# Prompt attention of a hybrid decoder: two heads in row halves of TensorE, probabilities weighted before their transposes, outputs summed in one PSUM bank

## The chip, the cores and the metric

The kernel runs as one program on one core of a Trainium2 chip. The metric is the device time in microseconds (us), the median of several runs. A profile of one execution goes with it; TensorE's granted clock is given there as a share of 2.4 GHz (0.50 is 1.2 GHz). All data is f32.

## The reference

One step through two trunk layers. Every layer runs two token mixers, on a prompt of 512 tokens and on a sample part of 8 sequences of 8 new tokens, then an MLP. What matters here is the prompt's attention:

```python
q_a, kv_c, kv_s, kv_w, gate, q_b, kv_b = _project(h, w_in)
kvc = _compress(kv_c, pe, w1, w2)                       # 31 compressed keys and values
o_cmp, o_sel = lax.map(lambda qp: _nsa_global(qp[0], qp[1], kvc, blocks, slopes_a), (qb, posb))
o_win, _ = _local_attn(q_a, kv_w[:, :, 0], kv_w[:, :, 1], slopes_a, WIN_A - 1, 1.0)
o_dil = _dilated_prompt(q_b, kv_b, slopes_b)
...
o_a = jnp.einsum('bthdc,bthc->bthd', o_a, gate)         # three branches, a gate for each
return jnp.concatenate([o_a.reshape(B, T, -1), o_dil.reshape(B, T, -1)], axis=-1) @ w_out
```

Eight sparse heads (two KV groups of four) attend to three sets of keys: compressed, selected and window. Each branch has its own softmax, and the three outputs are added with sigmoid gates. Eight dilated heads have one softmax each, whose bias holds the counts of the three dilations. Every score has an ALiBi bias. With 512 tokens every causal block is among the selected, so the selected branch is plain causal attention too.

## The kernel before

The order of work is written out by hand for each engine; engines meet at semaphores. A layer has the input projection, the prompt's attention, the sample part (8 batches), and the output projection with the MLP. The change lies in the prompt's attention.

It runs in four rounds (`g`). A round takes a pair of sparse heads (one of each KV group, 64 channels each, lying in the two halves of the 128 partitions) and a pair of dilated heads. Its 32 steps (`m`) are one head, one branch, one tile of 128 queries: 24 sparse (head 0 and head 1, each compressed, selected, window, four tiles each) and 8 dilated. Tile `t` sees 128 (t+1) keys; a compressed step has 32. GpSimd makes a copy of the pair's queries for each head, in which the other head's half is zero (`queries`), so that a score product over all 128 partitions gives one head.

A step goes through the engines thus. TensorE, `step_scores` (L1132): scores of up to 512 keys into bank `m % 2`. VectorE, `step_bias` (L1662): one pass adds the bias, stores the negated result to `p_sb` (four slots) and leaves the row minimum in `stat`. ScalarE (L673): exponential, with the row sum. TensorE, `step_transposes` (L1142, L1145): 128-column transposes into bank `2 + m % 2`. ScalarE (L683): copy to `p_pt`. TensorE, `step_outputs` (L1155, L1160): the transposed probabilities are stationary, and the values of both heads (128 columns) stream. VectorE, `step_add` (L1670 to L1686): reciprocal of the row sum, times the gate, and the head's 64 columns are added to `og` (or stored to `ogd`). TensorE's queue has scores(m), transposes(m-2), outputs(m-4). At a round's end eight transposes (`pair_transposes`, L1165) turn `og` and `ogd`, and VectorE copies them to `hT`.

VectorE makes the bias tables of the next part meanwhile (`sparse_bias` L1635, L1636; `dilated_bias` L1641). The sync queue loads the first window tiles (L502) once the projection is stored, and the dilated keys and values (L505 to L509) once `og_k` says that all pairs are kept. Then the sample part starts: L1229 compresses its pages, L1248 are the dilated scores.

## Time and profile before

| | us |
|---|---|
| median of 3 runs | 2600.89 (2598.64 to 2602.43) |
| profiled execution | 2606.01 |
| its span, first to last instruction | 2604.2 |
| TensorE busy in the span | 2444.6 |
| VectorE, ScalarE, GpSimd busy | 1007.6, 617.1, 504.0 |
| mean granted clock | 0.966 |

The span is what the trace covers; the execution's own time has some 2 us around it. A busy TensorE is an array with some matmul in it, not one at its peak: a matmul's record lasts from its start until its last column has left the array, so the starts of two neighbours show what it costs.

### The profile page before, as it was taken

What the parts mean: (1) busy time and instruction counts of PE and PEld (TensorE: products, weight loads), DVE (VectorE), ACT (ScalarE), POOL (GpSimd) and SP (SyncE); (2) the same over time, 40 slices, a digit from 0 to 9 for tenths busy, and PEclk for the clock granted to TensorE, in tenths of its full rate; (3) what the DMA queues carried; (4) which work ended last, traced back from release to release, by engine and by line L of the source; (5) the groups of instructions that cost most, each with busy time, mean ns of one, the idle gap of its engine ahead of it and who ended that gap; (6) DMA issues with size and microseconds to landing.
All of it is one profiled execution on the core that took longest, in us unless ns stands there. A gap on an engine that the chain in (4) does not pass through costs nothing.

```text
span 2604.2 us, 44706 instructions
## 1 busy us (share of the span) xinstructions
PE 2444.6 (94%) x13806; PEld 1755.5 (67%) x13806; DVE 1007.6 (39%) x3023; ACT 617.1 (24%) x1562; POOL 504.0 (19%) x511
## 2 busy tenths in 40 slices
PE   7998999898979999999999989999898789999998
PEld 4545777676756777777745466676676667777776
DVE  2002776434335332335500137753434352323374
ACT  2101555111112331221101026531111123232202
POOL 0001010000004343444200011100000233433340
PEclk8997999999989999999999979999999899999999
DMA  8633001787774344544365310037777553544541
GB/s 326 214 124 93 1 0 43 280 299 263 270 269 188 152 182 157 210 167 178 126 241 177 134 51 1 0 142 287 251 290 267 223 188 151 197 180 158 202 167 37
DMA packets 126229, 448.23 MB, mean 172 GB/s; under 512 B 17665, under 2 KB 89218, under 8 KB 104962
## 3 DMA queue, kind: packets, MB, share of 16 engines
q1 hardware_dynamic: 116464, 416.45, 43.3%
q10 hardware_dynamic: 9618, 29.98, 3.3%
q8 instruction: 72, 1.18, 0.2%
q14 instruction: 75, 0.61, 0.1%
HBM read 435.76 MB, written 152.57 MB: 226 GB/s over the span
## 4 chain that ended last, share of the span: by engine, by line
PE 84%; DVE 5%; issue 4%; DMA 4%; ACT 1%; SPq 1%; DVEq 0%; ACTq 0%; POOLq 0%
PE bank L969 35%; PE bank L1052 15%; PE bank L1229 8%; PE bank L1132 4%; DMA zone<-in_dilated_k 3%; PE bank L1160 3%; PE bank L1340 3%; PE bank L1248 2%; PE bank L1145 2%; PE bank L1373 1%; PE bank L1155 1%; PE bank L950 1%; DVE zone L1662 1%; PE bank L1068 1%; PE bank L1342 1%
## 5 line engine op out<-in xcount | busy, mean ns | idle before, releaser
L969 PE MATMUL bank<-zone,ring 128*128 128x288 f32 x1664 | 424.8, 407 | 8.0 <-DVE zone L1516 5.4
L1052 PE MATMUL bank<-ring,hT 128*128 128x512 f32 (+3 forms) x960 | 399.5, 571 | 7.9 <-ACTq L694 5.1
L969 PEld LDWEIGHTS bank<-zone,ring 128*128 128x128 f32 x1664 | 314.8, 190 | 101.0 <-DVE zone L1516 10.8
L969 PE MATMUL bank<-zone,w 128*128 128x288 f32 x1408 | 353.5, 406 | 0.0
L969 PEld LDWEIGHTS bank<-zone,w 128*128 128x128 f32 x1408 | 267.5, 190 | 73.9
L1052 PEld LDWEIGHTS bank<-ring,hT 128*128 128x128 f32 (+1 forms) x960 | 170.9, 183 | 204.2 <-issue 190.0
L1229 PE MATMUL bank<-ring,w 128*128 128x128 f32 x2048 | 239.6, 277 | 0.6 <-DMA ring<-in_cache_kv_cmp 0.6
L1229 PEld LDWEIGHTS bank<-ring,w 128*128 128x128 f32 x2048 | 232.1, 192 | 3.1 <-issue 2.4
L818 POOL TENSOR_TENSOR w<-ring 128x512 f32<-128x512 f32 x72 | 97.4, 1352 | 544.7 <-PE bank L969 310.9
L673 ACT ACTIVATE zone<-zone,stat 128x32 f32<-128x32 f32 (+4 forms) x256 | 128.4, 502 | 164.2 <-DVE stat L1662 162.2
L610 ACT COPY zone<-bank 128x288 f32<-128x288 f32 x72 | 28.7, 398 | 562.0 <-PE bank L969 562.0
L1132 PE MATMUL bank<-zone 128*128 128x512 f32 (+3 forms) x384 | 149.3, 472 | 0.2
L1160 PE MATMUL bank<-zone 128*128 128x128 f32 (+1 forms) x960 | 141.4, 279 | 0.3
L889 POOL TENSOR_TENSOR zone<-constants,stat 128x1024 f32<-128x1024 f32 x16 | 30.3, 1895 | 565.0 <-DVE stat L1860 565.0
L969 PE MATMUL bank<-xT,ring 128*128 128x288 f32 x512 | 135.2, 407 | 2.0 <-ACT zone L610 2.0
L1160 PEld LDWEIGHTS bank<-zone 128*128 128x128 f32 x960 | 123.0, 193 | 8.0 <-issue 6.8
L1662 DVE CUSTOM_DVE_ANT_0 zone<-bank,zone 128x32 f32<-128x32 f32 (+4 forms) x256 | 106.5, 416 | 35.9 <-PE bank L1132 22.2
L969 PEld LDWEIGHTS bank<-xT,ring 128*128 128x128 f32 x512 | 96.8, 190 | 29.3 <-ACT zone L610 2.9
L821 POOL TENSOR_TENSOR w<-w,ring 128x512 f32<-128x512 f32 x72 | 109.7, 1523 | 13.5 <-POOL w L818 13.5
L1248 PE MATMUL bank<-zone 128*32 128x128 f32 (+1 forms) x1664 | 67.8, 286 | 45.3 <-DMA zone<-in_dilated_k 45.3
L602 ACT ACTIVATE ring<-ring,gains 128x256 f32<-128x256 f32 x256 | 105.3, 495 | 0.0
L825 POOL TENSOR_TENSOR w<-ring,w 128x512 f32<-128x512 f32 x72 | 99.9, 1388 | 12.8 <-POOL ring L822 11.6
(240 smaller groups left out, 2890.9 us busy)
## 6 DMA issues: line engine op xcount, KB each, us to landing
out_dil_s<-in_state_kv_dil SPq DMA_DIRECT2D x48, 2720.0 KB, 12.0
ring<-in_w_units SPq DMA_DIRECT2D x72, 1024.0 KB, 4.8
zone<-in_dilated_v SPq DMA_DIRECT2D x16, 3328.0 KB, 11.2
ring<-in_cache_kv_cmp SPq DMA_DIRECT2D x256, 128.0 KB, 2.7
ring<-in_cache_kv_sel SPq DMA_DIRECT2D x256, 128.0 KB, 5.7
ring<-in_w_in SPq DMA_DIRECT2D x10, 2048.0 KB, 8.0
zone<-in_dilated_k SPq DMA_DIRECT2D x16, 1280.0 KB, 5.9
zone<-in_dilated_k SPq DMA_DIRECT2D x16, 1024.0 KB, 8.0
```

Of the source, the lines that this page charges most:

```text
L602: last = nc.scalar.activation(w_[:, h, k], w_[:, h, k], ACT.Copy, scale=gain_of(l * 2 + 1, 4 * h + k))
L673: nc.scalar.activation(p_sb[:, m % 4, 0:w], p_sb[:, m % 4, 0:w], ACT.Exp, scale=-1.0, bias=stat[:, 16 + m % 4:17 + m % 4], accum_out=stat[ ...
L818: nc.gpsimd.tensor_tensor(c_[:, 0], w_[:, 2], w_[:, 3], ALU.add).then_inc(s_comb.sem, 1)
L821: nc.gpsimd.tensor_tensor(c_[:, 1], c_[:, 0], w_[:, 0], ALU.subtract).then_inc(s_comb.sem, 1)
L825: nc.gpsimd.tensor_tensor(c_[:, 2], w_[:, 1], c_[:, 1], ALU.subtract).then_inc(s_comb.sem, 1)
L969: last = mm(dst[:, 0:HALF], lhs[:, k, :], rhs(k), start=first and k == 0, stop=(k == 3), skip_group_check=True)
L1052: last = mm(dst, hT[:, k, t * P:t * P + ROWS[t]], ring[:, n % 2, k * CH:k * CH + width], start=start and k == 0, stop=stop and k == KT - 1)
L1132: mm(bank[m % 2][:, 0:w], q[:, m % 4 * P:(m % 4 + 1) * P], kT[:, 0:w], start=True, stop=True).then_inc(a_s.sem, 1)
L1160: last = mm(dst, p_pt[:, m % 2, c * P:(c + 1) * P], v, start=(c == 0), stop=(c == w // P - 1))
L1229: last = mm(out[:, k, first:first + P], w1[:, s, j, :], rawt[:, :, s, k, j % 8, :], start=(j == 0 and k == 0), stop=(j == 15 and k == 1), ...
L1248: return mm(S[32 * g:32 * g + M, e * P:(e + 1) * P], strips[:, a, at:at + M], tile[:, p * P:(p + 1) * P], start=(j == 0 and p == 0), stop= ...
L1662: V.tensor_tensor_reduce(p_sb[:, m % 4, 0:w], bank[m % 2][:, 0:w], bias, -1.0, BIG, ALU.add, ALU.min, stat[:, 16 + m % 4:17 + m % 4]).then ...
```

## The change

A slot now has both heads of a pair, so a round has 12: selected, window and dilated, four tiles each. The two score products use 64 partitions each, at their own halves of the array's rows, and write to two banks; zeroed copies of the queries are gone. After the exponential VectorE takes the reciprocals of both row sums, and GpSimd multiplies the probabilities with reciprocal and gate (`weigh`) before they are transposed. ScalarE copies the first head's transposed probabilities, VectorE the second's; each head has one bank for them. For the outputs the values are stationary (128 rows, 64 columns) and the probabilities stream, the two heads at the two column halves; selected, window and compressed branch add up in bank 6, the dilated one is in bank 7, and ScalarE copies both to `hT` already turned. So `step_add` and `pair_transposes` go. The compressed branch of a pair is one block: four score products, softmax on 256 columns, four transposes, one output product of 512 columns. Its buffers lie where the projection was staged, so TensorE first waits for those stores, and the first window load waits for the end of the last round. 

```diff
-STEPS_A, STEPS_D = 24, 8
+STEPS_A, STEPS_D = 8, 4
 STEPS, ROUNDS = STEPS_A + STEPS_D, 4
-AHEAD = 4
+AHEAD, TO_T, TO_PV = 4, 3, 4
...
+        p_q, p_qd = part(10240, SEQ), part(10752, SEQ)
...
+        p_sb = part(W + 2048, 4, 2, SEQ)
+        p_kd = part(W + 7168, SEQ)
...
+        p_c, p_ptc, p_vd = part(stg_at, 4, 2, 32), part(stg_at + 256, SEQ, rows=slice(0, 64)), part(stg_at + 768, 4, P)
+        p_pt = [part(W + 6144, 2, SEQ), part(stg_at + 1280, 2, SEQ)]
...
+                sp.wait_ge(og_d.sem, og_d.at(l, ROUNDS))
                 load_window(0)
-                sp.wait_ge(og_k.sem, og_k.at(l, 8))
...
+            def step_probs(l, g, m):
+
+                n, w, slot = g * STEPS + m, step_keys(m), m % 4
+                for k in range(2):
+                    act.wait_ge(a_sb.sem, a_sb.at(l, 2 * n + k + 1))
+                    at = 2 * slot + k
+                    nc.scalar.activation(
+                        p_sb[:, slot, k, 0:w], p_sb[:, slot, k, 0:w], ACT.Exp, scale=-1.0,
+                        bias=stat[:, 16 + at:17 + at], accum_out=stat[:, 32 + at:33 + at]).then_inc(a_e.sem, 1)
+
+            def keep_first_head(l, g, m):
+
+                n, w = g * STEPS + m, step_keys(m)
+                act.wait_ge(a_t.sem, a_t.at(l, 2 * n + 1))
+                if not isinstance(n, int) or n >= 2:
+                    act.wait_ge(a_o.sem, a_o.at(l, n - 1))
+                copy(p_pt[m % 2][:, 0, 0:w], bank[4][:, 0:w]).then_inc(a_pt[0].sem, 1)
...
+                        step_probs(l, *in_round(g, m))
+                    if m == 6:
+                        act.wait_ge(c_b.sem, c_b.at(l, g + 1))
+                        nc.scalar.activation(p_c, p_c, ACT.Exp).then_inc(c_e.sem, 1)
+                    if m >= TO_T and (m - TO_T < STEPS or not ends):
+                        keep_first_head(l, *in_round(g, m - TO_T))
+                    if m == 9:
+                        act.wait_ge(c_t.sem, c_t.at(l, g + 1))
+                        copy(p_ptc, bank[7][low, :]).then_inc(c_k.sem, 1)
+                    if m == 11:
+                        keep_pair(l, g, g, bank[6], STEPS_A).then_inc(og_a.sem, 1)
+                    if m == STEPS + TO_PV - 1:
+                        keep_pair(l, g, g + 4, bank[7], STEPS).then_inc(og_d.sem, 1)
...
+                def weigh(g, m):
+
+                    n, w, slot = g * STEPS + m, step_keys(m), m % 4
+                    pool.wait_ge(a_w.sem, a_w.at(l, n + 1))
+                    pool.sem_inc(waits_taken_pool, 1)
...
+                        p = p_sb[:, slot, k, 0:w]
+                        inverse = sm[:, 2 * slot + k:2 * slot + k + 1]
+                        if m < STEPS_A:
+                            last = nc.gpsimd.tensor_scalar(p, p, inverse, p_gate[:, m % 4, k, 1 + m // 4:2 + m // 4],
+                                                           ALU.mult, ALU.mult)
+                        else:
+                            last = nc.gpsimd.tensor_scalar(p, p, inverse, None, ALU.mult)
+                        last.then_inc(a_n.sem, 1)
...
+                    for m in range(STEPS):
+                        weigh(g, m)
+                        if m == 1:
+                            pool.wait_ge(a_s.sem, a_s.at(l, g * STEPS))
+                            pool.sem_inc(waits_taken_pool, 1)
+                            pair_copy(p_kd, kbT[:, ds(g, 1), :])
+                            pair_copy(p_qd, qbT[:, ds(g, 1), :]).then_inc(a_q.sem, 1)
+                        if m == 3:
+                            pool.wait_ge(a_o.sem, a_o.at(l, g * STEPS))
+                            pool.sem_inc(waits_taken_pool, 1)
+                            nc.gpsimd.tensor_copy(p_vd, vst[:, :, ds(256 + g * P, P)]).then_inc(a_q.sem, 1)
+                        if m == 6:
+                            pool.wait_ge(c_w.sem, c_w.at(l, g + 1))
+                            pool.sem_inc(waits_taken_pool, 1)
+                            nc.gpsimd.tensor_tensor(
+                                p_c.rearrange("p t k n -> p (t k) n"), p_c.rearrange("p t k n -> p (t k) n"),
+                                sm[:, 56:64].unsqueeze(2).to_broadcast([P, 8, NCK_P]), ALU.mult).then_inc(c_n.sem, 1)
+                        if m == 9 and more:
+                            pool.wait_ge(a_s.sem, a_s.at(l, g * STEPS + STEPS_A))
+                            pool.sem_inc(waits_taken_pool, 1)
+                            pair_copy(p_q, qaT[:, ds(g + 1, 1), :]).then_inc(a_q.sem, 1)
+
...
+                n, w, t = g * STEPS + m, step_keys(m), m % 4
+                q, kT = (p_q, (ksT, kwT)[m // 4]) if m < STEPS_A else (p_qd, p_kd)
...
+                for k, rows in enumerate((low, high)):
+                    last = mm(bank[2 * (m % 2) + k][:, 0:w], q[rows, t * P:(t + 1) * P], kT[rows, 0:w], start=True, stop=True)
+                last.then_inc(a_s.sem, 1)
+
+            def step_transposes(l, g, m):
+
+                n, w, slot = g * STEPS + m, step_keys(m), m % 4
+                for k in range(2):
+                    pe.wait_ge(a_n.sem, a_n.at(l, 2 * n + k + 1))
+                    if not isinstance(n, int) or n >= 1:
+                        pe.wait_ge(a_pt[k].sem, a_pt[k].at(l, n))
                     pe.sem_inc(waits_taken_pe, 1)
+                    for c in range(w // P):
+                        last = tr(bank[4 + k][:, c * P:(c + 1) * P], p_sb[:, slot, k, c * P:(c + 1) * P], ident[:])
+                    last.then_inc(a_t.sem, 1)
...
+                for c in range(w // P):
+                    for k, rows in enumerate((low, high)):
+                        if m < STEPS_A:
+                            at = m // 4 * P + k * HD
+                            v, B, first = vst[:, c, at:at + HD], bank[6], m == 0
+                        else:
+                            v, B, first = p_vd[:, c, k * HD:(k + 1) * HD], bank[7], m == STEPS_A
+                        last = mm(B[rows, t * P:(t + 1) * P], v, p_pt[m % 2][:, k, c * P:(c + 1) * P], start=first and c == 0,
+                                  stop=(c == w // P - 1), skip_group_check=True)
                 last.then_inc(a_o.sem, 1)
...
+                    last = mm(bank[7][:, t * 64:(t + 1) * 64], p_q[:, t * P:(t + 1) * P], ktcp[:].rearrange("p k n -> p (k n)"),
+                              start=(t == 0), stop=(t == 3), skip_group_check=True)
...
+                    last = tr(bank[7][low, t * P:(t + 1) * P], p_c[:, t].rearrange("p k n -> p (k n)"), ident[:])
...
+                mm(bank[6][:], vcp[:], p_ptc, start=False, stop=True, skip_group_check=True)
...
+                    if m == 5:
+                        chunk_scores(l, g)
+                    if m >= TO_T and (m - TO_T < STEPS or not ends):
+                        step_transposes(l, *in_round(g, m - TO_T))
+                    if m == 9:
+                        chunk_probs_transposes(l, g)
+                    if m >= TO_PV:
+                        step_outputs(l, g, m - TO_PV)
+                    if m == 10:
+                        chunk_outputs(l, g)
...
+                for k in range(2):
+                    at = 16 + 2 * slot + k
+                    V.tensor_tensor_reduce(
+                        p_sb[:, slot, k, 0:w], bank[2 * (m % 2) + k][:, 0:w],
+                        (p_bias if m < STEPS_A else p_biasd)[:, k, SEQ - w:SEQ], -1.0, BIG,
+                        ALU.add, ALU.min, stat[:, at:at + 1]).then_inc(a_sb.sem, 1)
...
+                out, sums = sm[:, 2 * slot:2 * slot + 2], stat[:, 32 + 2 * slot:34 + 2 * slot]
+                V.reciprocal(out, sums).then_inc(a_w.sem, 1)
...
+                V.tensor_copy(p_pt[m % 2][:, 1, 0:w], bank[5][:, 0:w]).then_inc(a_pt[1].sem, 1)
...
+                V.tensor_tensor(v, bank[7][:, 0:256].rearrange("p (a n) -> p a n", a=8),
+                                p_biasc.rearrange("p t k n -> p (t k) n"), ALU.add).then_inc(order.sem, 1)
...
+                V.tensor_reduce(sm[:, 40:48], v, X, ALU.max).then_inc(order.sem, 1)
...
+                V.tensor_tensor(v, v, sm[:, 40:48].unsqueeze(2).to_broadcast([P, 8, NCK_P]), ALU.subtract).then_inc(c_b.sem, 1)
...
+                V.tensor_reduce(sm[:, 48:56], p_c.rearrange("p t k n -> p (t k) n"), X, ALU.add).then_inc(order.sem, 1)
...
+                V.reciprocal(sm[:, 48:56], sm[:, 48:56]).then_inc(order.sem, 1)
...
+                V.tensor_tensor(sm[:, 56:64], stat[:, 40:64].rearrange("p (a e) -> p a e", e=3)[:, :, 0], sm[:, 48:56], ALU.mult).then_inc(c_w.sem, 1)
...
+                    if m >= 1 and (m - 1 < STEPS or not ends):
+                        step_weights(l, *in_round(g, m - 1))
...
+                    if m == 5:
+                        chunk_bias(l, g, order)
+                    if m == 7:
+                        chunk_weights(l, g, order)
...
+                    if m >= TO_T and (m - TO_T < STEPS or not ends):
+                        keep_second_head(l, *in_round(g, m - TO_T))
```

**The order on TensorE.** A sparse step whose scores have 512 keys, before (names: `bank` is PSUM, `zone` the work buffer in SBUF; a row of a matmul against f32 data is two records in the trace):

```order
L1132 MATMUL bank<-zone 128x512 [waits scores_biased]
L1145 MATMUL bank<-c_ident,zone 128x128 [waits probsT_kept,probs]
L1145 MATMUL bank<-c_ident,zone 128x128
L1160 MATMUL bank<-zone 128x128 [waits outputs_added,probsT_kept]
L1160 MATMUL bank<-zone 128x128 x3
```

And now the slot of such scores, with the end of the slot before it ahead:

```order
L1212 MATMUL bank<-zone 64x128 x5
L1177 ISA
L1180 MATMUL bank<-zone 128x512 [waits scores_biased]
L1180 MATMUL bank<-zone 128x512
L1187 ISA
L1189 REGISTER_ALU [waits probs_weighted]
L1192 MATMUL bank<-c_ident,zone 128x128 [waits first_head_kept]
L1187 ISA
L1192 MATMUL bank<-c_ident,zone 128x128 [waits probs_weighted,second_head_kept]
L1212 MATMUL bank<-zone 64x128 [waits first_head_kept,second_head_kept]
L1212 MATMUL bank<-zone 64x128 x7
```

The next score product stands behind outputs that wait for both copies; the transposes are now those of m-3, and wait for GpSimd's `probs_weighted` and for the copy of the step before.

**The order on VectorE.** The step with 384 keys, before, in a sparse branch:

```order
L1660 ISA [waits probs_transposed]
L1662 ISA zone,stat<-bank,zone 128x384 [waits scores]
L1662 ISA stat 128x1
L1670 RECIPROCAL sm<-stat 128x1 [waits outputs]
L1671 ISA
L1681 ISA [waits vector_order_prompt]
L1681 TENSOR_TENSOR sm<-sm,gate 128x1
L1682 ISA
L1686 SCALAR_TENSOR_TENSOR zone<-bank,sm,zone 128x64 [waits vector_order_prompt]
```

And now:

```order
L1725 ISA [waits probs_transposed]
L1729 ISA zone,stat<-bank,zone 128x384 [waits scores]
L1729 ISA stat 128x1
L1729 ISA zone,stat<-bank,zone 128x384
L1729 ISA stat 128x1
L1737 ISA
L1740 RECIPROCAL sm<-stat 128x2 [waits probs]
L1747 REGISTER_ALU [waits probs_transposed]
L1748 COPY zone<-bank 128x512 [waits outputs]
```

Two biasing passes stand in a row, the reciprocal waits for ScalarE's exponential in place of the outputs, and a copy of transposed probabilities takes the place of the gate product and the accumulation.

## Rows read from the trace of the kernel before

**Rows 1.** TensorE's timeline where the stage begins and ends (start, duration, us).

```profile
253.29 1.03 PE L1132 MATMUL bank<-ktcp,zone 128*128 128x32 f32 x4 [0.69 <-DVE zone L1773]
...
446.73 2.51 PE L1229 MATMUL bank<-ring,w 128*128 128x128 f32 x21
```

**Rows 2.** Busy time per engine of the stage (PE, PEld, DVE, ACT, POOL), clock, DMA.

```profile
253.00:447.00 194.00, 180.74 (x1107) 136.25 (x1108) 139.81 (x642) 110.92 (x384) 16.88 (x18) 0.95 0.00 1
```

**Rows 3.** Chain of waits in the stage: the same product, two rounds apart.

```profile
289.54 0.89 PE bank L1160 x8
...
383.57 0.89 PE bank L1160 x8
```

**Rows 4.** TensorE's timeline, the four steps of a dilated tile row.

```profile
430.06 0.39 PE L1132 MATMUL bank<-zone 128*128 128x128 f32 x2
...
431.27 0.61 PE L1145 MATMUL bank<-c_ident,zone 128*128 128x128 f32 x4
431.72 0.61 PE L1160 MATMUL bank<-zone 128*128 128x128 f32 x4
...
434.67 1.06 PE L1160 MATMUL bank<-zone 128*128 128x128 f32 x8
435.57 0.39 PE L1132 MATMUL bank<-zone 128*128 128x128 f32 x2
```

**Rows 5.** Timeline: a 512-key score product and VectorE's pass behind it.

```profile
439.54 1.02 PE L1132 MATMUL bank<-zone 128*128 128x512 f32 x2
...
440.40 0.38 PE L1145 MATMUL bank<-c_ident,zone 128*128 128x128 f32 x2
...
440.75 0.69 DVE L1662 CUSTOM_DVE_ANT_0 zone<-bank,zone 128x512 f32<-128x512 f32 x1 [0.97 <-PE bank L1132]
```

**Rows 6.** Sample part: 32 records on alternating column halves, and the next.

```profile
487.49 1.97 PE L1373 MATMUL bank<-ring,zone 128*64 128x128 f32 x32
489.38 0.43 PE L1377 MATMUL bank<-vsm,zone 64*64 64x128 f32 x2
```

**Rows 7.** Sample part: products on 128 columns, then one on 64.

```profile
508.41 0.66 PE L1278 MATMUL bank<-w,zone 128*128 128x64 f32 x4
509.00 0.32 PE L1285 MATMUL bank<-zone,q_s 128*64 128x128 f32 x1
```

**Rows 8.** VectorE's groups in the stage (count | busy us, mean ns | idle before).

```profile
L1670 DVE RECIPROCAL sm<-stat 128x1 f32<-128x1 f32 x128 | 20.6, 161 | 15.5 <-PE bank L1160 13.8 <-PE bank L1155 0.5
...
L1662 DVE CUSTOM_DVE_ANT_0 zone<-bank,zone 128x512 f32<-128x512 f32 x24 | 16.6, 692 | 8.8 <-PE bank L1132 8.7
...
L1662 DVE CUSTOM_DVE_ANT_0 zone<-bank,zone 128x256 f32<-128x256 f32 x24 | 10.2, 425 | 1.0 <-issue 0.5 <-PE bank L1132 0.2
...
L1662 DVE CUSTOM_DVE_ANT_0 zone<-bank,zone 128x128 f32<-128x128 f32 x24 | 7.0, 291 | 2.1 <-PE bank L1145 0.7 <-PE bank L1132 0.5 <-issue 0.5
...
L1641 DVE SCALAR_TENSOR_TENSOR zone<-constants 128x512 f32<-128x512 f32 x8 | 5.7, 748 | 0.2
```

**Rows 9.** ScalarE's groups in the stage.

```profile
L673 ACT ACTIVATE zone<-zone,stat 128x512 f32<-128x512 f32 x24 | 17.3, 722 | 22.2 <-DVE stat L1662 22.2
...
L683 ACT COPY zone<-bank 128x512 f32<-128x512 f32 x24 | 13.7, 571 | 1.4 <-PE bank L1160 1.3
L673 ACT ACTIVATE zone<-zone,stat 128x256 f32<-128x256 f32 x24 | 12.2, 508 | 14.0 <-DVE stat L1662 13.7
L683 ACT COPY zone<-bank 128x384 f32<-128x384 f32 x24 | 11.0, 460 | 0.1
```

**Rows 10.** GpSimd's groups over the span.

```profile
L818 POOL TENSOR_TENSOR w<-ring 128x512 f32<-128x512 f32 x72 | 97.4, 1352 | 544.7 <-PE bank L969 310.9 <-ACT ring L602 224.8 <-DMA ring<-in_w_units 9.0
...
L839 POOL COPY zone<-zone 128x512 f32<-128x512 f32 x8 | 4.9, 618 | 200.2 <-ACT zone L657 200.2
```

**Rows 11.** Busy time and granted clock (third last) at the stage's start.

```profile
250.00:260.00 10.00, 5.53 (x22) 4.13 (x22) 6.54 (x24) 2.37 (x13) 2.95 (x3) 0.50 0.00 1
260.00:270.00 10.00, 10.00 (x25) 5.90 (x26) 5.58 (x24) 3.83 (x14) 0.00 (x0) 0.50 0.00 0
270.00:280.00 10.00, 9.84 (x72) 8.56 (x70) 6.59 (x35) 5.72 (x22) 0.00 (x0) 0.93 0.01 3
```

**Rows 12.** A DMA issue (KB, us to landing); first batch's wait for dilated keys.

```profile
zone<-in_window_tiles SPq DMA_DIRECT2D x16, 512.0 KB, 3.5
...
469.55 1.94 PE L1248 MATMUL bank<-zone 128*32 128x128 f32 x32 [2.47 <-DMA zone<-in_dilated_k]
```

More of the change, by code:

```diff
@@ L89 @@
 ND_TILES, ND_A = 13, 5
-CH_L, CH_A, CH_S = 6, ROUNDS * (2 * STEPS_A + STEPS_D), 13
+CH_L, CH_A, CH_S = 6, ROUNDS * 4, 13
 def step_keys(m):
-    if m < STEPS_A and m % 12 < 4:
-        return NCK_P
     return (m % 4 + 1) * P
@@ L323, in build @@
         g_exp = ev("gates_exp", NT)
-        g_rdy = ev("gates_ready", 2)
+        g_rdy = ev("gates_ready", 3)
         slot_n = [0] * STG
@@ L677, in prompt_steps @@
-                    if m >= 2 and (m - 2 < STEPS or not ends):
-                        w = step_keys((m - 2) % STEPS)
-                        act.wait_ge(a_t.sem, a_t.at(l, n - 1))
-                        if m >= 4:
-                            act.wait_ge(a_o.sem, a_o.at(l, n - 3))
-                        R, cols = (NCK_P, P) if w == NCK_P else (P, w)
-                        copy(p_pt[0:R, m % 2, 0:cols], bank[2 + m % 2][0:R, 0:cols]).then_inc(a_pt.sem, 1)
+                        step_probs(l, *in_round(g, m))
@@ L1216, in _ @@
                 pe.wait_ge(sg_rdy.sem, sg_rdy.at(l, 2))
+                for s in range(STG):
+                    pe.wait_ge(z_out[s].sem, z_out[s].at(l, slot_n[s]))
                 pe.sem_inc(waits_taken_pe, 1)
@@ L1645, in step_bias @@
             def step_bias(l, g, m):
[L1647 to L1653 removed]
+                n, w, slot = g * STEPS + m, step_keys(m), m % 4
                 if m == 0:
@@ new lines, in step_bias, with step_weights @@
+                for k in range(2):
+                    at = 16 + 2 * slot + k
[3 more added lines that the diff above has]
+                        ALU.add, ALU.min, stat[:, at:at + 1]).then_inc(a_sb.sem, 1)
+            def step_weights(l, g, m):
+                n, slot = g * STEPS + m, m % 4
+                dve.wait_ge(a_e.sem, a_e.at(l, 2 * n + 2))
+                dve.sem_inc(waits_taken_dve, 1)
+                out, sums = sm[:, 2 * slot:2 * slot + 2], stat[:, 32 + 2 * slot:34 + 2 * slot]
+                V.reciprocal(out, sums).then_inc(a_w.sem, 1)
@@ L1781, in _ @@
                 sparse_bias(0)
-                for m in range(AHEAD):
-                    step_bias(l, 0, m)
+                prompt_steps(l, 0, 0, AHEAD, False)
                 with dve.Fori(0, ROUNDS - 1) as g:
```

239 lines of the change are left out of this document (93 added, 146 removed).

## The prediction

> **What bounds the kernel now.** I began with the busy time by stretch. The stage that the change rewrites is the prompt attention of each layer. In layer 0 it begins with the score product at 253.29 and ends where TensorE takes the first product of the sample part at 446.73 [rows 1]: 193.4 us. TensorE is busy for 180.7 of 194 us there, VectorE for 139.8, ScalarE for 110.9, GpSimd for 16.9, and next to nothing moves by DMA [rows 2]. The stage runs twice, so a microsecond saved in one of its four rounds counts eight times. One round takes 47.0 us (two periods between the same product at 289.54 and 383.57 [rows 3]); four are 188, and 5.4 us remain for the two ends.
>
> The dilated part shows the stage at its best: four steps, 128 to 512 keys, take 430.06 to 435.57, 5.5 us, with TensorE never idle [rows 4]. A transpose costs 0.112 us (four in 0.45 us), a product record of 128 columns the same (eight in 0.90), and every f32 product is two records. A score product against 512 keys takes 0.86 us from its start to the next transpose [rows 4, 5]. So the stage is bound by TensorE's columns, with the chain of small steps around them. The sample part and the MLP aren't touched.
>
> **The change, part by part.** Per round there are now 12 slots instead of 32 steps; a slot has both heads of a pair. Three groups of four slots (128, 256, 384, 512 keys) do the same 24 wide steps; the eight compressed steps become one block.
>
> *TensorE.* Scores: same columns, but the two heads use different row halves. If they run side by side, a group costs 0.22 + 0.43 + 0.65 + 0.86 = 2.2 us; in turn, 4.3. The trace has no pair of row halves. Its nearest rows are column halves: 32 records of 128 columns take 487.49 to 489.38, 0.059 us each, against 0.112 alone [rows 6]. I take side by side, and keep "in turn" for the range. Transposes: 20 x 0.112 = 2.25 us. Outputs: 40 records on alternating column halves, the very form of rows 6, 40 x 0.059 = 2.4 us where they now take 4.5. Then there is a cost that the diff doesn't name. A slot uses the array as 64 rows by 128 columns, as 128 by 128, and as 128 by 64. The four records at 508.41 are followed only after 0.59 us by the first product on 64 columns [rows 7], where four records cost 0.45 [rows 4]: 0.14 us for a change of shape. Three per slot are 12 x 0.14 = 1.7 us a group.
>
> The Trainium skill, TensorEngine Tiling, Key Properties, says that a change of tiling mode drains the engine; that speaks against this change, and the 0.14 us agrees with it. By that rule the group is 8.5 us, without it 6.8.
>
> The sum of a group is 2.2 + 2.25 + 2.4 + 1.7 = 8.5 us, 25.6 a round. The compressed block adds eight records (0.9), four transposes (0.45), one 512-column product (0.86) and four changes (0.6): 2.8. TensorE: 28.4 us a round. The eight closing transposes of a round are gone.
>
> *VectorE.* Two biasing passes per slot, mean (0.69 + 0.29) / 2 = 0.49 us [rows 8]; one reciprocal, 0.16 plus 0.04 to the next; one copy out of PSUM, for which I take the same 0.49. A group: 3.9 + 0.8 + 2.0 = 6.7 us, a round 20.1. The bias tables are four wide passes of at most 0.75 [rows 8] and two narrow ones, 3.6; the block's three passes and a sum over 256 columns (0.42 each, by the pass of 256 keys) with two small ones 2.1. Together 25.8 us. The per-step reciprocal, gate product and accumulation of before are gone.
>
> *ScalarE.* 24 exponentials, 0.56 at the mean width of 320, and 12 copies, 0.41 there [rows 9], with one exponential and three 512-wide copies: 13.5 + 4.9 + 2.2 = 20.6 us.
>
> *GpSimd* gets work it never had: 24 multiplies a round with a scalar per row. No row shows that operation. Lower end: a 512-wide copy at 0.62 us; upper end: a two-input pass at 1.35 [rows 10]. A mean width of 320 makes 24 multiplies 9 to 20 us; with four copies and the small ones (3.5) 13 to 24 us. I take 18. Even the upper end is under TensorE's 28.4, and a weight has two slots until its transposes ask for it, so it costs nothing; it would from some 1.9 us for 512 keys on (24 x 1.9 x 320/512 + 3.5 = 32 us).
>
> *The chain through the queues.* Sums alone don't give the round. TensorE's queue has scores(m), transposes(m-3), outputs(m-4); the transposed probabilities of a head have one bank, so these transposes wait until ScalarE and VectorE have copied out m-4, and ScalarE copies that only after the exponentials of m-1. Only after the outputs does the next score product come, and VectorE waits for it. Followed from the end of the 256 biasing: exponential 0.51, copy of 384 0.46 [rows 9], eight transposes 0.90, outputs of 384 0.71, three changes 0.42, scores of 512 0.86, hand-over to VectorE 0.35 (scores issued by 440.40, pass begins at 440.75 [rows 5]), two passes of 512 1.38, ScalarE to TensorE about 0.15: 5.7 us for two slots. The same chain through the other two slots: 0.72 + 0.25 + 0.45 + 0.24 + 0.42 + 0.43 + 0.35 + 0.84 + 0.15 = 3.9. A group is then 9.6 us, longer than TensorE's 8.5 and VectorE's 6.7; three are 28.8, and the compressed block's 2.8 us stand in the same queue: **31.6 us a round**, against 47.0.
>
> *The ends.* Four rounds are 126.4 us. I keep the 5.4 us of the ends. In the first 18 us of the stage the granted clock is 0.50, that is 1.2 GHz, and it rises to 0.93 in the ten after that, once TensorE has been busy without a gap [rows 11]. The old stage spent this on small compressed steps; the new one begins with wide ones, where TensorE's 28 us a round would be near 50. I add 4 us. Stage: 136 us, 57.4 less.
>
> *The window load.* The sync queue now issues the first window load (512 KB, 3.5 us to landing) behind the end of the stage and ahead of the dilated keys, and a product already waits 2.47 us for these [rows 12]. From 0 to 3.5 us a layer; I take 1.5, 3 us in all. The additional waits of TensorE for the stores of the projection cost nothing: those were issued 20 us earlier, and 14 us of products lie between.
>
> **Sum.** 2 x 57.4 - 3 = 112 us. The profiled execution took 2606.0 us; 2494. The median of the runs is 5.1 us under that execution: **2489 us**.
>
> **Rivals.**
> - Row halves one after the other. For it: no row shows them side by side. The chain gains 0.43 + 0.86 a group (10.9), TensorE's own sum becomes 34.8; about 36 us a round, stage 154, 2 x 39.4 - 3 = 76 saved: 2525 us.
> - The changes of shape hidden behind the waits for the copies, or a shorter hand-over: 28.5 us a round with the chain at 8.8, stage 123; 2 x 70.0 - 3 = 137 saved, 2464 us. At the floor, VectorE's 25.8, stage 113: 2442. Against it: the chain is the longest, and the changes stand on it.
> - Slower than before: the clock doesn't come back. Every duration of TensorE doubles but the changes: (28.4 - 6.2) x 2 + 6.2 = 51 less the overlap of small records, some 48 us a round. TensorE is then the bound, 4 x 48 + 4 = 196 us against 193.4; with the window load 8 us more, 2609 us. The point is a round of 47 us. For it: these 18 us at 0.50 now, and more gaps in the new stage. Against it: at 0.50 TensorE would have no gap at all, and in just that state the clock rose [rows 11]. The Trainium skill, TensorE: Matmul & The Clock Gate, Part 4, holds that transposes don't count as busy the same way; the stretch in which the clock rose had them between its products, so the trace bears it out poorly.
> - GpSimd's multiply at twice its upper end, 2.7 us for 512 keys: 24 x 1.7 + 3.5 = 44 us a round, stage 185, 2587 us. Its price is not in the trace, but no one-input row comes near.
>
> **How the numbers follow.** The forecast (30 to 34 us a round, 2476 to 2508) has a chance of 0.53; the shorter round 0.18, row halves in turn 0.14, the low clock 0.05, GpSimd 0.04, others (a wait I haven't seen, at either side) 0.06. The range 2445 to 2540 takes in the second and third case. A difference of 0.2%, 5 us, is about what a measurement of this kernel tells from no change. Faster 0.90, same 0.03, slower 0.07: the low clock, and a part of the unseen.
>
> **What the profile after would show.** Side by side: the second head's 512-key records start within the first head's, and a 512 score pair takes 0.9 us, not 1.7. The changes: gaps of 0.14 us between a slot's three kinds of product. The chain: VectorE waiting for scores, TensorE for the first head's copy, the 512 slots longest. GpSimd: multiplies of 0.6 to 1.4 us, idle between. Clock: 0.50 no longer than some 20 us into the stage. A period of 30 to 34 us. It is wrong if GpSimd or the clock becomes the bound, or if row halves don't overlap.

## The result, and the profile after

The changed kernel takes 2477.56 us (median of four runs, 2469.47 to 2480.55) against 2599.76 us for the kernel before: ratio 0.9526, 95% interval 0.9500 to 0.9552. It is 122 us faster; the forecast was 112 and 2489 us, its range 2445 to 2540. The profiled execution took 2477.39 us.

TensorE's timeline, at the beginning and the end of the first layer's stage (answers to [rows 1]):

```profile
254.51 1.65 PE L1180 MATMUL bank<-zone 64*128 64x128 f32 x8 [1.18 <-DVE sgate L1864]
...
390.65 1.05 PE L1300 MATMUL bank<-ring,w 128*128 128x128 f32 x7
```

The stage is 136.1 us, and 136.2 in the second layer, where it was 193.4 and 193.0. Busy time per engine (PE, PEld, DVE, ACT, POOL), granted clock third last, for the stage ([rows 2]) and for its first 30 us ([rows 11]):

```profile
254.00:391.00 137.00, 120.64 (x971) 75.97 (x972) 87.98 (x338) 78.76 (x256) 89.61 (x121) 0.95 0.00 1
254.00:264.00 10.00, 7.19 (x29) 3.61 (x30) 6.94 (x32) 5.81 (x22) 4.63 (x9) 0.62 0.00 1
264.00:274.00 10.00, 10.00 (x58) 6.70 (x56) 5.66 (x18) 3.76 (x12) 4.66 (x7) 0.66 0.01 2
274.00:284.00 10.00, 8.73 (x81) 5.83 (x81) 7.76 (x31) 6.23 (x21) 5.83 (x8) 1.00 0.00 1
```

TensorE, VectorE and ScalarE all lost work; GpSimd went from 17 to 90 us. One group of four slots on TensorE's timeline (answers to [rows 4, 5]; scores L1180, transposes L1192, outputs L1212):

```profile
326.18 1.13 PE L1180 MATMUL bank<-zone 64*128 64x512 f32 x4
327.24 0.44 PE L1192 MATMUL bank<-c_ident,zone 128*128 128x128 f32 x2
327.61 1.10 PE L1212 MATMUL bank<-zone 128*64 128x128 f32 x16
328.63 0.49 PE L1180 MATMUL bank<-zone 64*128 64x128 f32 x4
330.06 0.73 PE L1192 MATMUL bank<-c_ident,zone 128*128 128x128 f32 x4 [0.94 <-ACT zone L673]
330.79 0.44 PE L1212 MATMUL bank<-zone 128*64 128x128 f32 x4
331.16 0.70 PE L1180 MATMUL bank<-zone 64*128 64x256 f32 x4
331.79 1.11 PE L1221 MATMUL bank<-ktcp,zone 128*128 128x64 f32 x8
332.73 0.83 PE L1192 MATMUL bank<-c_ident,zone 128*128 128x128 f32 x6
333.49 0.66 PE L1212 MATMUL bank<-zone 128*64 128x128 f32 x8
334.08 0.92 PE L1180 MATMUL bank<-zone 64*128 64x384 f32 x4
```

Read it by starts. The pair of 512-key score products takes 327.24 - 326.18 = 1.06 us, of which 0.14 is the change of shape behind it by the prediction's reading, and 16 output records take 1.02. There is one gap in the group, 0.94 us, where the transposes wait for ScalarE's copy of a first head. The 512-key product of one round starts at 326.18 and that of the next at 358.06: a round of 31.9 us, in which TensorE is busy for 28.7. VectorE meanwhile waits for just the product at 326.18:

```profile
327.51 0.69 DVE L1729 CUSTOM_DVE_ANT_0 zone<-bank,zone 128x512 f32<-128x512 f32 x1 [1.34 <-PE bank L1180]
```

The waits of the stage, summed (engine, line, what for: us in total, times, longest):

```profile
ACT zone L663 <- DVE stat L1729: 55.2, 40, 6.0
...
DVE zone L1729 <- PE bank L1180: 31.4, 37, 2.1
...
PE bank L1192 <- ACT zone L673: 12.6, 16, 1.4
...
PE bank L1192 <- POOL zone L874: 1.5, 3, 0.8
```

GpSimd's groups in the stage ([rows 10]); L871 multiplies the sparse probabilities by two scalars, L874 the dilated ones by one:

```profile
L871 POOL TENSOR_SCALAR zone<-zone,sm,stat 128x512 f32<-128x512 f32 x16 | 15.9, 1003 | 1.3 <-DVE sm L1740 1.2
...
L874 POOL TENSOR_SCALAR zone<-zone,sm 128x512 f32<-128x512 f32 x8 | 12.4, 1564 | 0.0
```

### The profile page after: what moved, and what is told of

Same layout as the page of the kernel before. It is cut to its first block, busy times and chain, and to the rows that moved or that the text cites. A ratio compares the mean times of both kernels' runs of the same rounds, so it can differ in the third digit from the quotient of the medians.

```text
span 2475.6 us, 43070 instructions
## 1 busy us (share of the span) xinstructions
PE 2310.8 (93%) x13534; PEld 1626.9 (66%) x13534; DVE 901.8 (36%) x2423; ACT 553.4 (22%) x1306; POOL 643.0 (26%) x719
## 4 chain that ended last, share of the span: by engine, by line
PE 83%; DVE 5%; issue 5%; DMA 4%; ACT 1%; DVEq 0%; POOL 0%; ACTq 0%; SPq 0%; POOLq 0%
PE bank L1020 36%; PE bank L1103 16%; PE bank L1300 9%; DMA zone<-in_dilated_k 4%; PE bank L1411 3%; PE bank L1180 2%; PE bank L1192 2%; PE bank L1319 2%; PE bank L1212 2%; PE bank L1444 1%; PE bank L1001 1%; ACT zone L663 1%; PE bank L1119 1%; PE bank L1413 1%; PE bank L1428 1%
## 5 line engine op out<-in xcount | busy, mean ns | idle before, releaser
L663 ACT ACTIVATE zone<-zone,stat 128x128 f32<-128x128 f32 (+1 forms) x192 | 106.2, 554 | 110.2 <-DVE stat L1729 110.2
L1020 PEld LDWEIGHTS bank<-xT,ring 128*128 128x128 f32 x512 | 97.0, 190 | 29.3 <-ACT zone L601 2.9
L1729 DVE CUSTOM_DVE_ANT_0 zone<-bank,zone 128x128 f32<-128x128 f32 (+1 forms) x192 | 86.5, 488 | 69.7 <-PE bank L1180 63.1
L871 POOL TENSOR_SCALAR zone<-zone,sm,stat 128x128 f32<-128x128 f32 (+3 forms) x128 | 85.3, 677 | 90.2 <-DVE sm L1740 90.0
L1192 PE MATMUL bank<-c_ident,zone 128*128 128x128 f32 x480 | 78.6, 289 | 29.9 <-ACT zone L673 25.1
L1192 PEld LDWEIGHTS bank<-c_ident,zone 128*128 128x128 f32 x480 | 53.3, 146 | 77.8 <-issue 75.5
```

What stands on the lines that cost most here:

```text
L663: nc.scalar.activation(p_sb[:, slot, k, 0:w], p_sb[:, slot, k, 0:w], ACT.Exp, scale=-1.0, bias=stat[:, 16 + at:17 + at], accum_out=stat[:, ...
L871: last = nc.gpsimd.tensor_scalar(p, p, inverse, p_gate[:, m % 4, k, 1 + m // 4:2 + m // 4], ALU.mult, ALU.mult)
L1020: last = mm(dst[:, 0:HALF], lhs[:, k, :], rhs(k), start=first and k == 0, stop=(k == 3), skip_group_check=True)
L1192: last = tr(bank[4 + k][:, c * P:(c + 1) * P], p_sb[:, slot, k, c * P:(c + 1) * P], ident[:])
L1729: V.tensor_tensor_reduce(p_sb[:, slot, k, 0:w], bank[2 * (m % 2) + k][:, 0:w], (p_bias if m < STEPS_A else p_biasd)[:, k, SEQ - w:SEQ], -1 ...
```

## The experiments

The kernel before ran beside each of three groups of kernels: 2601.74 us beside kernels 1 to 4, 2596.66 beside 5 to 8, 2595.89 beside 9 to 12. The ratios are to these. The theory is the chain of the prediction. A round is 28.4 us of TensorE's own work plus the wait of the transposes for ScalarE's copy, which hangs on the 512 and 384 scores. The rivals are those on record.

**1 and 2. Do the halves run side by side?** Both heads' scores on the lower row half, or both heads' outputs on the lower column half; either leaves a part of the second head out of what is computed.

```diff
# rows_in_turn
-                    last = mm(bank[2 * (m % 2) + k][:, 0:w], q[rows, t * P:(t + 1) * P], kT[rows, 0:w], start=True, stop=True)
+                    last = mm(bank[2 * (m % 2) + k][:, 0:w], q[low, t * P:(t + 1) * P], kT[low, 0:w], start=True, stop=True)
# cols_in_turn
-                        last = mm(B[rows, t * P:(t + 1) * P], v, p_pt[m % 2][:, k, c * P:(c + 1) * P], start=first and c == 0,
+                        last = mm(B[low, t * P:(t + 1) * P], v, p_pt[m % 2][:, k, c * P:(c + 1) * P], start=first and c == 0,
```

> Both heads' score products use the lower row half (the second head is scored with the first head's channels), so they have to run one after the other. My theory (the row halves run side by side, and scores stand on the chain that sets a round): the 256 and 512 score pairs cost 0.43 and 0.86 us more on the chain, TensorE's own sum becomes 35 us; a round of 36 us in place of 31.9, stage about 153, 2512 us. Rival (scores are hidden behind the waits for the copies): a round under 33 us, at most 8 us more than the changed kernel's 2477.6.

> Both heads' output products go to the lower column half, so they have to run one after the other (the second head's outputs are added to the first's). My theory: outputs of a group of four slots cost 40 x 0.112 = 4.5 us where they cost 2.4; TensorE's sum of a group rises to 10.6 us and passes the chain (9.6 plus 0.95): a round of 34.5 us, 2.6 more than now, 2498 us. Rival (outputs are off the chain, since VectorE is what binds): under 5 us more.

Measured: rows in turn 2527.46 us (ratio 0.9722, interval 0.9673 to 0.9771), rounds of 36.7 to 36.8 us, stages of 158.1 and 167.0; columns in turn 2513.53 (0.9653, 0.9633 to 0.9674), rounds of 35.1, stages of 150.7 and 149.6. Both took some 15 us more than expected. TensorE's timeline of rows in turn, then of columns in turn:

```profile
328.79 1.98 PE L1180 MATMUL bank<-zone 64*128 64x512 f32 x4
330.70 0.44 PE L1192 MATMUL bank<-c_ident,zone 128*128 128x128 f32 x2
```

```profile
334.81 1.13 PE L1180 MATMUL bank<-zone 64*128 64x512 f32 x4
335.87 0.44 PE L1192 MATMUL bank<-c_ident,zone 128*128 128x128 f32 x2
336.24 1.96 PE L1212 MATMUL bank<-zone 128*64 128x128 f32 x16
```

The same 512 pair takes 1.91 us from start to next start on one row half and 1.06 on two; the 16 outputs have a record of 1.96 us in place of 1.10. So the halves do run side by side, in rows and in columns, and the rival "row halves in turn" is the first kernel, 50 us slower than the changed one. Not all of these 50 us are the score products: in its second layer the granted clock stayed at 0.50 for the first 41.1 us of the stage, with TensorE busy all the time in the second half of that:

```profile
1503.00:1523.00 20.00, 20.00 (x80) 12.13 (x79) 7.88 (x31) 6.92 (x22) 6.14 (x9) 0.50 0.01 2
```

Columns in turn add 3 x 40 x (0.112 - 0.059) = 6.4 us of TensorE to a round, and the round grows by 3.2 only: most of the rest went into TensorE's idle time, which falls from 3.2 to 0.4 us a round. So TensorE's own work is not the bound of the changed kernel, but near it.

**3. Is the wait the chain?** TensorE issues the scores of the next slot ahead of the outputs of this one.

```diff
-                    if m < STEPS or not ends:
-                        step_scores(l, *in_round(g, m))
+                    if m == 0:
+                        step_scores(l, g, 0)
...
+                    if m + 1 < STEPS or not ends:
+                        step_scores(l, *in_round(g, m + 1))
```

> Everything is kept, but TensorE issues the scores of slot m+1 between the transposes of m-3 and the outputs of m-4, in place of behind these outputs. My theory (VectorE waits 31 us of a stage for scores because these stand behind outputs that wait for both copies): outputs leave the chain, and TensorE's own sum of 28.4 us binds; a round of 29 to 30 us, about 18 us less in all, 2460 us. Rival (the wait only moves, since the scores now stand behind the transposes that wait for the copies all the same): a round of 31 to 32 us, within 6 us of the changed kernel.

**4. The other end of the chain.** ScalarE's copy stands between its two exponentials, not behind both.

```diff
-                        step_probs(l, *in_round(g, m))
+                        step_probs(l, *in_round(g, m), (0,))
+                    if m >= TO_T and (m - TO_T < STEPS or not ends):
+                        keep_first_head(l, *in_round(g, m - TO_T))
+                    if m < STEPS or not ends:
+                        step_probs(l, *in_round(g, m), (1,))
```

> Everything is kept, but ScalarE copies the first head's transposed probabilities between the two exponentials of a slot, in place of after both. My theory (the copy behind the second exponential is a link of the chain; TensorE sits idle up to 0.94 us for it): the chain loses an exponential of 0.4 to 0.7 us in every second slot; a round of 29 to 30 us, 2460 us. Rival (the copy now waits for transposes that are not yet done and holds up the second exponential): a round as long as now or longer, 2477 us or more.

**5. Both.**

> Both reorderings in one kernel: the scores of the next slot are issued ahead of the outputs of this one, and ScalarE's copy of the first head lies between its two exponentials. By the chain theory (what the unchanged round pays beyond TensorE's own work is the wait for the 512 and 384 products), with the scores a slot earlier there is no chain left in the round and TensorE's own sum, 28.4 us with its changes of shape, decides: scores_ahead already ran 29.3 us per round, so this one gives 28.5 to 29.2 us, a stage of 123 to 126 us and about 2452 us. Rival: the two effects add (0.9 us off 29.3 us and more), which TensorE's sum would not allow if it is right: 28.0 us or less and 2445 us. Second rival: the copy now holds up the second exponential, and the round is 29.5 us or more, 2462 us.

Measured: scores ahead 2457.04 us (0.9442, 0.9421 to 0.9464), rounds 29.3, stages 126.1 and 126.2. Copy between 2472.19 (0.9489, 0.9461 to 0.9517), round 31.0, where 29 to 30 was expected; stages 129.6 and 132.3. Both together 2454.31 (0.9447, 0.9417 to 0.9476), rounds 28.34, stages 119.4 and 119.4. The chain is shown: a reordering that leaves the durations as they were to some 1% (the 512-key exponential 714 ns in the changed kernel and 723 with both edits, its copy 564 and 566) takes the wait away. TensorE's idle time in a round falls from 3.2 us to 1.0 with the scores ahead, 2.0 with the copy between and 0.1 with both. Where ScalarE copies earlier, a part of the wait moves, for one to VectorE's copy of the second head:

```profile
336.02 0.41 PE L1194 MATMUL bank<-c_ident,zone 128*128 128x128 f32 x2 [0.23 <-ACT zone L673]
337.00 0.41 PE L1194 MATMUL bank<-c_ident,zone 128*128 128x128 f32 x2 [0.58 <-DVE zone L1750]
```

With both edits the round stops at the sum that the prediction made for TensorE, 28.4 us; that the two add up to 28.0 or less did not happen. The sum is nearly right in its parts too. In this kernel, without waits, a group with the compressed block's score products in it (L1223) reads

```profile
312.77 1.13 PE L1182 MATMUL bank<-zone 64*128 64x512 f32 x4
...
318.05 1.10 PE L1223 MATMUL bank<-ktcp,zone 128*128 128x64 f32 x8
318.99 0.82 PE L1194 MATMUL bank<-c_ident,zone 128*128 128x128 f32 x6
...
322.20 1.13 PE L1182 MATMUL bank<-zone 64*128 64x512 f32 x4
```

which is 9.43 us, and 8.49 without the block's 0.94, where 8.5 was forecast. The same group of the changed kernel, 326.18 to 336.75, takes 10.57, and 9.63 without the block's 0.94, where the chain was to give 9.6. The block's three parts are 2.5 us a round (2.8 forecast), which leaves 8.6 us for the mean group of both edits and 9.8 for that of the changed kernel. The stage of both edits, 119.4 us, is shorter than the 123 to 126 expected, and not by its rounds: what a stage has beyond four rounds fell from 8.7 us with the scores ahead to 6.0, while the half clock in it fell from 13.5 us to 6.7.

**6 and 7. What does a change of shape cost?** One product of a single column more per slot, between the transposes of the two heads: over all 128 rows as they are, or over 64.

```diff
# tiny_same_shape
+                    if k == 1:
+                        mm(bank[5][:, 0:1], ident[0:P, :], ident[0:P, 0:1], start=True, stop=True, skip_group_check=True)
# tiny_other_shape
+                    if k == 1:
+                        mm(bank[5][:, 0:1], ident[low, :], ident[low, 0:1], start=True, stop=True, skip_group_check=True)
```

> One more product of a single column in each slot, between the transposes of the first and of the second head, over the same 128 rows as they: it changes no shape. It is the control of the next kernel. One record more of some 0.06 us per slot (one per slot, 8 slots in a round): 0 to 0.5 us per round, so a round of 31.8 to 32.4 us and 2478 to 2482 us.

> The same product of one column at the same place, but over the lower 64 rows: the array's shape changes before it and after it, two changes more in each slot. The prediction took 0.14 us per change. If a change costs that wherever it stands, and TensorE's own time is on the round's path, the round is longer than in tiny_same_shape by 16 x 0.14 = 2.2 us (8.5 us per stage, 17 us in all: about 2497 us). Where the change hides behind the wait for the 512 product, the difference is under half of that: under 2488 us. Rival: a change of shape costs nothing and the gap that I read is the wait of the output products for their operands: no difference beyond 3 us.

Those texts count eight slots to a round; it has twelve, so the difference to expect was 24 x 0.14 = 3.4 us. Measured: 2487.60 us (0.9567, 0.9519 to 0.9616) and 2509.66 (0.9680, 0.9636 to 0.9724), rounds of 32.9 and 34.9, stages of 141.6 and 151.0. TensorE's timelines, same shape and then other shape:

```profile
325.06 0.55 PE L1194 MATMUL bank<-c_ident,zone 128*128 128x128 f32 x3
325.44 0.28 PE L1192 MATMUL bank<-c_ident 128*128 128x1 f32 x2
325.58 0.52 PE L1194 MATMUL bank<-c_ident,zone 128*128 128x128 f32 x3
```

```profile
318.55 0.55 PE L1194 MATMUL bank<-c_ident,zone 128*128 128x128 f32 x3
319.03 0.38 PE L1192 MATMUL bank<-c_ident 64*128 64x1 f32 x2
319.34 0.55 PE L1194 MATMUL bank<-c_ident,zone 128*128 128x128 f32 x3
```

From the one set of transposes to the other it is 0.52 us, or 0.79 with the shape changed and changed back: 0.135 us for one change, if the two cost the same. The trace has 0.10 of the 0.27 between the two records of the small product, whose shape is one, so it prices the way there and back and not each change. The 24 changes should cost 3.2 us a round. The round is 2.0 longer and TensorE's idle time falls by 0.8 (from 2.3 to 1.5), which makes 2.8, or 0.117 for one: at some places a change costs less. The control cost 1.0 us a round, twice what I had expected at most, since its product is two records and takes 0.14 us (325.44 to 325.58) where I had counted 0.06.

**8. The multiply's form.**

```diff
-                            last = nc.gpsimd.tensor_scalar(p, p, inverse, None, ALU.mult)
+                            last = nc.gpsimd.tensor_scalar(p, p, inverse, 1.0, ALU.mult, ALU.mult)
```

> GpSimd's multiply of the dilated probabilities gets a second scalar of 1.0 and so the form with two multiplies; the numbers stay the same. In the unchanged kernel the form with two scalars took 1003, 661, 555 and 487 ns for 512, 384, 256 and 128 columns, the form with one 1564, 1242, 922 and 758 ns. If the form decides, the dilated multiplies fall to the former times, GpSimd's busy time in a round from 22.4 to some 18 us, the round itself stays at 31.8 us (GpSimd isn't on its path), and each stage's end is about 0.5 to 1 us shorter: 2476 us, within 3 us of the unchanged kernel. Rival: the place decides (which half of the row's engines is busy beside it), and the durations stay at 1.5 us for 512 columns.

Measured: 2475.12 us (0.9533, 0.9502 to 0.9564), which by the totals is the changed kernel again, but the stages are 133.3 and 134.7 us, and the round 31.5 to 31.6. GpSimd's group:

```profile
L874 POOL TENSOR_SCALAR zone<-zone,sm 128x512 f32<-128x512 f32 x8 | 5.5, 696 | 0.1
```

The form decides: 696 ns where it was 1564, at the same place. GpSimd was on the path after all, a little inside a round (31.9 to 31.6 us), and more at the end. In the changed kernel TensorE ends a stage by waiting three times for L874:

```profile
385.08 0.52 PE L1192 MATMUL bank<-c_ident,zone 128*128 128x128 f32 x3 [0.17 <-POOL zone L874]
385.53 0.66 PE L1212 MATMUL bank<-zone 128*64 128x128 f32 x8
386.72 0.63 PE L1192 MATMUL bank<-c_ident,zone 128*128 128x128 f32 x4 [0.53 <-POOL zone L874]
388.16 0.63 PE L1192 MATMUL bank<-c_ident,zone 128*128 128x128 f32 x4 [0.81 <-POOL zone L874]
```

From the last 512-key product to the stage's end it is 11.9 us there and 10.0 in this kernel. So the form is worth 1.9 us at the end and 0.3 in each round, some 3 us a stage; the first layer's stage shows 2.8. The second layer's shows 1.5, with 18.6 us of half clock in it where the changed kernel had 13.2.

**9 and 10. The edits that helped, and the queue place of the window load.** The second kernel adds to the first:

```diff
-                load_window(0)
                 load_dilated_k(0)
                 load_dilated_v(0)
+                load_window(0)
```

> Three edits together: scores a slot ahead, ScalarE's copy between the two exponentials, and the dilated multiply in the form with two scalars. The first two gave rounds of 28.34 us, TensorE's own sum (28.4 us), so the third can't shorten the round any more: 28.3 us. In dilated_two_scalars the stages were 133.3 and 134.7 us against 136.1 and 136.2, of which 0.3 to 0.4 us per round came from the round and the rest from the end. So here some 0.5 to 1.5 us per stage from the end alone: stages of 118 to 119 us, and 2451 us, by the phase of the half-clock stretches outside the stage 2443 to 2460. Rival: nothing at all is left at the end (the last multiply hides behind products), stages of 119.4 us as in ahead_and_between.

> As best_three, and the first window load is issued behind the dilated keys and values of the sample part instead of ahead of them. In the changed kernel the first batch's products waited 3.31 us for the dilated keys against 2.47 us before; I took 1.5 us per layer for this queue place and the trace shows 0.84. With the keys first, that wait falls by 0.5 to 1 us per layer, if the window itself is needed later: 1 to 2 us in all, under what a comparison of totals can tell, so the wait in the profile decides. Rival: the window is then what the first batch waits for, and the sum of both waits is the same.

Measured: 2441.83 us (0.9404, 0.9372 to 0.9435) and 2444.59 (0.9416, 0.9387 to 0.9445); stages of 118.1 and 118.2 us in both. The three edits together are 36 us faster than the changed kernel beside them (2477.76 us, kernel 11), and the stages of these two profiles differ by 37.0. Of these the eight rounds are 28, the rest lies at the stages' beginning and end: there GpSimd no longer holds TensorE up, and the half clock at the beginning is 6.7 and 6.9 us where it was 18.1 and 13.5. How much the shorter half clock is worth was not separated. The stage in the first, all engines:

```profile
245.00:363.00 118.00, 115.53 (x969) 72.38 (x969) 88.64 (x337) 80.32 (x255) 71.71 (x121) 0.97 0.00 1
```

TensorE is now busy for 98% of it. The window load's place does nothing that shows: the first batch waits 3.58 and 2.84 us for its dilated keys in one kernel, 3.35 and 2.83 in the other.

**11 and 12. The time outside the stages.** Both kernels once more, unchanged, for their profiles.

> The changed kernel once more, unchanged. The time outside the two stages was 2198.6 us in its first profile and 2217.8 us in that of the kernel before, 19 us that no line of the change touches, with 134 us of half clock in all; over my variants, whose edits don't touch it either, it went from 2194.0 to 2214.6 us. Theory (the half-clock stretches outside the stage fall on other work from one execution to the next): the stages are 136.1 us again within 0.3 us, and the time outside them differs from 2198.6 by several us, anywhere from 2194 to 2216. Rival (it is fixed by the program, and so a gain of the change): 2198.6 us again within 1.5 us.

> The kernel before once more, unchanged, for a second profile. Same theory: stages of 193.2 us within 0.5 us, and the time outside them not 2217.8 us again but several us away, with the half-clock stretches at other places; above all the compression products ahead of the second layer's stage (3.6 us per sixteen at half clock in the first profile) need not run at half clock. Rival: the same stretches at the same places, 2217.8 us within 1.5 us.

Measured: the changed kernel 2477.76 us (0.9540, 0.9517 to 0.9564), the kernel before 2597.24 in its one profiled execution. The 2217.8 us in these texts took the whole span; to TensorE's last instruction, as for the other numbers, it is 2213.6. All in us, from the profiles:

| kernel | stages | of each at half clock | time outside them | of it at half clock |
|---|---|---|---|---|
| before | 193.4, 193.0 | 18.2, 17.7 | 2213.6 | 138.2 |
| before, again | 193.4, 192.7 | 18.1, 17.0 | 2205.1 | 115.1 |
| changed | 136.1, 136.2 | 14.0, 13.2 | 2198.6 | 102.5 |
| changed, again | 137.1, 136.1 | 18.1, 13.5 | 2198.5 | 98.1 |
| rows in turn | 158.1, 167.0 | 20.1, 41.1 | 2193.0 | 88.9 |
| copy between | 129.6, 132.3 | 7.2, 14.7 | 2214.6 | 135.1 |
| two scalars | 133.3, 134.7 | 13.6, 18.6 | 2194.0 | 90.7 |
| both orders | 119.4, 119.4 | 6.8, 6.6 | 2211.6 | 130.0 |
| best three | 118.1, 118.2 | 6.7, 6.9 | 2194.1 | 82.0 |

The changed kernel repeated its 2198.6 us, against my theory and as the rival said; the kernel before did not. One of its stages was a microsecond longer, against the 0.3 expected, and had 18.1 us of half clock. The two layers of "copy between" and of "rows in turn" differ in the same way: the layers run the same code, and the one with more half clock takes longer. So a stage compares two kernels to a few us only, and a round at full clock to 0.1. Over all 14 profiles, though, the time outside the stages goes with the half clock in it: a line of 0.39 us per us of half clock, correlation 0.96. That is a correlation; no run changed the clock alone. The place of it moved as well. Ahead of the second layer's stage, clock third last, in the first profile of before and in the second:

```profile
1514.00:1533.00 19.00, 16.54 (x82) 15.53 (x80) 3.64 (x15) 0.63 (x2) 0.70 (x1) 0.50 0.41 124
```

```profile
1509.00:1528.00 19.00, 15.79 (x116) 11.77 (x114) 5.29 (x21) 1.31 (x3) 2.61 (x3) 0.93 0.49 146
```

## Why the prediction was right, and where it was off

**The stage.** Forecast 57.4 us less in each layer; measured 57.3 and 56.8. The round was to be 31.6 us and is 31.8 to 31.9; the ends were to be 9.4 and are 136.1 - 4 x 31.87 = 8.6. VectorE's sum was too high (25.8 us a round, busy for 21.8), ScalarE's nearly right (20.6 and 19.7); neither set the round.

**The chain.** Its place was named before and is where the trace has the wait. TensorE waits 12.6 us in a stage for ScalarE's copy, 3.15 a round, and is busy for 28.7 of the 31.88. Moving either end shortened the round (kernels 3 to 5), with TensorE's sum left at 28.34. The group was to take 9.6 us by the chain; the one shown takes 9.63, the mean 9.8.

**TensorE's terms.** Side by side is shown by kernels 1 and 2. The rival's price, 2525 us, met 2527 by luck: its stages were to be 154 us and are 158.1 and 167.0, and the time outside them is the least of all profiles. The change of shape was read off one gap, 0.14 us, and is 0.135 by the gap in kernel 7, 0.117 over its round. The Trainium skill, TensorEngine Tiling, Key Properties, says that a changed tiling mode drains the engine. The trace agrees as far as a change costs time.

**GpSimd.** The step that failed is "I take 18 ... so it costs nothing". It is 22.4 us a round, inside the bounds, because the one-scalar form takes 1.56 us for 512 keys, above the "upper end" of 1.35. And nothing is not its price: TensorE waits 1.5 us for it at the stage's end, where no later slot covers it, and by kernel 8 the slow form costs some 3 us a stage, 1.9 of them at the end. The condition "two slots until its transposes ask for it" held inside a round but for 0.3 us.

**The window load.** I took 1.5 us a layer. The first batch waited for its dilated keys 2.47 and 4.03 us in one profile of before and 4.37 and 4.19 in the other, 3.31, 3.28, 3.90 and 3.98 in those of the changed kernel. In both orders, with the load at the same place, it waited 4.67 and 4.82. The one row in [rows 12] was the lowest of four. In this spread no cost of the load shows, and moving it (kernel 10) left the wait as it was.

**The clock.** The rival in which it stays low did not come: 0.62 and 0.66 in the stage's first two stretches of 10 us, then 1.00, with gaps on TensorE in all of the stage. But the argument against it, that without gaps the clock rises, was too strong: in the second layer of rows in turn TensorE was busy for 20 of 20 us at 0.50, and the clock came back only 41.1 us into the stage.

**The total.** It was 10 us better than forecast (122 against 112). The window load is 3 of them, the stages -0.7. The other 8 lie outside the stages, where no term of the prediction stands for them: that is luck. The profiles have 2209.4 us there before and 2198.6 after, means of two, 10.8 less for 26.4 us less half clock; by the 0.39 that would be 10.3. So the half clock goes with all of it, by a correlation. Whether the changed kernel always has less of it, or these four profiles happened to, stays open: its two agree, but variants that share its code outside the stage span 2193 to 2215 us.

**Two sums that don't come out.** The changes of shape in the low-clock rival are 3 x 1.7 + 0.6 = 5.7 us a round, not 6.2; its 51 us stay. The shorter round with a chain of 8.8 is 3 x 8.8 + 2.8 = 29.2 us, not 28.5, and its total 2470, not 2464.

## What to carry to other kernels

Make two sums for a software-pipelined stage: each engine's work, and the chain through the queues in the order in which they are issued. Where the chain is longer, issue the producer of its longest link a slot earlier before making anything faster; here this was worth some 21 us alone and 36 together with two small edits. Before setting a cost to zero because two slots cover it, look at the last slots of the stage. Compare rounds at full clock, and look at the half clock in a stage before reading its length. And where one row is to carry a term, look whether its twin in the other layer says the same.

## What the runs showed of the hardware

- GpSimd's tensor_scalar was slower with one scalar than with two: 1564, 1242, 922 and 758 ns for 512, 384, 256 and 128 columns, against 1003, 661, 555 and 487 with two scalars from SBUF, and 696, 587, 482 and 525 with the second an immediate 1.0. Why was not tried.
- A change of TensorE's shape from 128x128 to 64x128 and back cost 0.27 us in one slot, 0.135 for each, and 0.117 for each over a round (kernel 7). From 128x128 to 128x64 it was 0.14 in the trace of before [rows 7].
- Two f32 products of 512 columns on the two row halves run side by side: the pair takes 1.06 us with one change of shape, and 1.91 on one half.
- Half-clock stretches outside the stage differed between executions of one kernel by up to 23 us (138.2 and 115.1), and a us of them went with some 0.4 us of time over 14 profiles. At a stage's beginning it came to 6.6 to 41.1 us in all, and to 20.1 and 41.1 in the two stages of one profile (rows in turn).
